# Sixteen gate tiles of block 1 moved to the first four turns, with later turns and a closer-packed norm

## The reference

```
h = RMSNorm(x);  P = h @ W_in     # q, k, v, og, low-rank decays, glu (value, gate), gA, gB
yA = (RMSNorm per head of GLA(q, k, v) * silu(og)) @ W_o
u  = glu_value * sigmoid(glu_gate)
yB = silu(LayerNorm(conv31(u))) @ W_pw2          # 31 taps, depthwise
x  = x + (sigmoid(gA) * yA + sigmoid(gB) * yB) @ W_out
x  = x + PEER(RMSNorm(x));  out = RMSNorm(x)
```

## Time and profile before

| | us |
|---|---|
| median of 3 runs | 4311.64 |
| lowest, highest | 4308.58, 4317.77 |
| the profiled execution, its own time | 4304.48 |
| its span in the trace | 4302.7 |

### The profile page before, as it was taken

How to read it: one execution, slowest core, us unless ns; L and a number is a source line. 1 busy time by engine, 2 the same in 40 slices (tenths; PEclk the granted TensorE clock), 3 DMA queues, 4 the chain that set the end, 5 groups by cost and what they waited for, 6 DMA issues and landing times. The chain is left out here.

```text
span 4302.7 us, 39452 instructions
## 1 busy us (share of the span) xinstructions
PE 3720.1 (86%) x13650; PEld 2238.9 (52%) x13650; DVE 2660.2 (62%) x3879; ACT 878.4 (20%) x2022; POOL 775.2 (18%) x525
## 2 busy tenths in 40 slices
PE   9999999999999989676799697858898887777777
PEld 3444489446666676573788586334444442322222
DVE  3232368103899999965777877876666664544444
ACT  2233210101122221241111111122222222212112
POOL 0000000000233323322221311321211121212111
PEclk9999999999999999898899898879999999999999
DMA  3111258888899999999999999999999999999998
GB/s 134 59 59 59 73 183 302 301 314 308 345 385 406 392 412 415 411 395 410 426 425 426 417 418 427 426 416 426 416 428 428 428 415 426 425 429 428 428 429 373
DMA packets 136877, 1530.03 MB, mean 356 GB/s; under 512 B 15297, under 2 KB 15425, under 8 KB 15937
## 3 DMA queue, kind: packets, MB, share of 16 engines
q0 software_dynamic: 73728, 1073.77, 59.3%
q1 hardware_dynamic: 61488, 445.33, 26.9%
q10 hardware_dynamic: 1552, 9.57, 0.6%
HBM read 1524.42 MB, written 4.19 MB: 355 GB/s over the span
## 5 line engine op out<-in xcount | busy, mean ns | idle before, releaser
L1773 PE MATMUL bank<-arena_h,wring 128*128 128x128 f32 (+5 forms) x6656 | 1384.0, 371 | 122.4 <-DVE arena_h L1471 41.7
L1773 PEld LDWEIGHTS bank<-arena_h,wring 128*128 128x128 f32 x6656 | 1026.0, 196 | 479.5 <-issue 188.5
L633 POOL DMA_INDIRECT arena_c<-in_peer_uv,arena_c x256 | 511.3, 1997 | 2469.7 <-DVE arena_o L1403 1320.0
L1394 DVE SCALAR_TENSOR_TENSOR arena_c<-arena_c 128x2048 f32<-128x2048 f32 x256 | 585.3, 2286 | 183.4 <-DMA arena_c<-in_peer_uv,arena_c 183.2
L2165 PE MATMUL bank<-arena_c,arena_h 128*128 128x512 f32 x1020 | 475.9, 610 | 156.7 <-ACT arena_h L1000 156.7
L1403 DVE SCALAR_TENSOR_TENSOR arena_o<-arena_c,arena_o 128x2048 f32<-128x2048 f32 x234 | 549.4, 2348 | 45.3 <-ACT arena_c L803 39.3
L2132 PE MATMUL bank<-arena_c,cols 128*128 128x512 f32 x1024 | 470.4, 602 | 95.8 <-ACT cols L958 93.8
L1670 DVE SCALAR_TENSOR_TENSOR arena_c<-arena_c 128x2048 f32<-128x2048 f32 x128 | 293.4, 2292 | 332.4 <-DMA arena_c<-in_peer_uv,arena_c 332.3
L801 ACT ACTIVATE arena_c<-arena_c 128x1 f32<-128x1 f32 x384 | 77.9, 203 | 1919.8 <-DVE arena_c L1394 1428.7
L646 POOL DMA_INDIRECT arena_c<-in_peer_uv,arena_c x256 | 261.8, 1023 | 1032.6 <-PE bank L2132 523.8
L1614 DVE SCALAR_TENSOR_TENSOR arena_c<-arena_c 128x2048 f32<-128x2048 f32 x128 | 293.4, 2292 | 238.7 <-DMA arena_c<-in_peer_uv,arena_c 237.8
(11 more groups left out here) (237 smaller groups left out, 2617.7 us busy)
## 6 DMA issues: line engine op xcount, KB each, us to landing
wring<-in_w_in SPq DMA_DIRECT2D x176, 1024.0 KB
wring<-in_w_out SPq DMA_DIRECT2D x48, 1024.0 KB
wring<-in_peer_w_q SPq DMA_DIRECT2D x48, 1024.0 KB
wring<-in_gla_w_o SPq DMA_DIRECT2D x32, 1024.0 KB
wring<-in_conv_w_pw SPq DMA_DIRECT2D x32, 1024.0 KB
wring<-in_w_v SPq DMA_DIRECT2D x16, 1024.0 KB
wring<-in_w_ga SPq DMA_DIRECT2D x16, 1024.0 KB
wring<-in_w_o_quarters SPq DMA_DIRECT2D x16, 1024.0 KB
```

Source lines behind the costliest of these rows:

```text
L633: pool.indirect_dma_start(out=slot_of(n), out_offset=None, in_=uv_tab, in_offset=at)\
L1394: V.scalar_tensor_tensor(row, row, 1.0, block_of(h2, n // P), ALU.mult, ALU.mult, accum_out=act_u[:, n % TOP:n % TOP + 1]).then_inc(dotted, 1)
L1773: last = M(ps[bank][:, at:at + hi - lo], w_tile(slot)[:, k, :], act_in[:, k, lo:hi], start=k == 0, stop=k == KT - 1)
```

## The change

- **Loads and TensorE.** Right after the first glu tiles come eight second gate tiles (`SB_GB0`, pairs 0 to 3), into banks 4 to 7, and then turn 0's output gates. Each of turns 0 to 3 keeps its pair (now pairs 4 to 7). The eight tiles between the last turn and the pointwise tiles are gone. So ten are made in turn 0 and two in each of turns 1 to 3.
- **Turns.** Turn 0 begins at step 6 instead of 4 and has 17 steps instead of 11; turns 1 to 3 begin 8 steps later with unchanged lengths (12, 11, 12); turns 4 to 7 have 9, 9, 8, 8 steps instead of 9, 9, 9, 8. The last tap falls before step 92 instead of 85.
- **Turn 0's places.** Its output gates are scaled at steps 8 and 11 of the turn. ScalarE's sigmoids of pairs 0 to 3 stand at steps 7 to 10, those of pairs 4 to 7 at the step of the second scaling.
- **Norm.** Subtractions and squares take two steps instead of four, four pairs of tiles and eight tiles a step. `RSTD_AT` is 6 steps after the last turn's end (7 before), the pointwise merges 8 (10), the residual additions 15, 16, 17, 18 (18, 20, 22, 24), the norm 19 (25), the queries 24 (30), the search 26 (32).
- **Semaphores.** TensorE waits for the sigmoids of banks 4 to 7 ahead of each output-gate tile, and at the end of a turn for that turn's sigmoid.

```diff
+SB_GB0 = SB_GLU1 + 4
+SB_OG1 = SB_GB0 + 8
...
-TURN_AT = (4, 15, 27, 38, 50, 59, 68, 77, 85)
+TURN_AT = (6, 23, 35, 46, 58, 67, 76, 84, 92)
 OG_AT = (4, 7)
+OG_AT_FIRST = (8, 11)
 IT_AT = (2, 5)
-X1_AT = 84
-GB_IN_TURN = 7
-GB_AT = (84, 86)
-XC_AT, SQUARE_AT = 88, 89
-RSTD_AT = 92
-PW_AT = 95
-SCALE2_AT, SILU2_AT = 96, 97
-RES1_AT = (103, 105, 107, 109)
-NORM1_AT = 110
-QUERY1_AT = 115
-FIND_AT = 5
+X1_AT = 91
+GB_FIRST_AT = (7, 8, 9, 10)
+XC_AT, SQUARE_AT = 95, 96
+RSTD_AT = 98
+PW_AT = 100
+SCALE2_AT, SILU2_AT = 101, 102
+RES1_AT = (107, 108, 109, 110)
+NORM1_AT = 111
+QUERY1_AT = 116
+FIND_AT = 6
...
             loads(SB_GLU1 + 2, 0, 4, w_in, WGLU, 2)
+            loads(SB_GB0, 0, 8, w_in, WGB, 8)
...
-                    loads(first + 4, i, 20, w_in, i * 4 + (WGB + 2 * turn), 2)
+                    loads(first + 4, i, 20, w_in, i * 4 + (WGB + 8 + 2 * turn), 2)
...
-            loads(SB_GB1, 0, 8, w_in, WGB + 8, 8)
...
-                A(sgb1[:, 2 * n:2 * n + 2, :], two(4 if n < 4 else 6 + n % 2, P), ACT.Sigmoid).then_inc(p["sig"], 1)
+                A(sgb1[:, 2 * n:2 * n + 2, :], two(4 + n if n < 4 else 4, P), ACT.Sigmoid).then_inc(p["sig"], 1)
...
-                    if j < 4 and r + 1 in OG_AT:
-                        og1_silu(j, OG_AT.index(r + 1))
-                    if j < 4 and r == GB_IN_TURN:
-                        mb1_gates(j)
+                    og_at = OG_AT if j else OG_AT_FIRST
+                    if j < 4 and r + 1 in og_at:
+                        og1_silu(j, og_at.index(r + 1))
+                    if j < 4 and r == og_at[1]:
+                        mb1_gates(4 + j)
...
-                if s in GB_AT:
-                    mb1_gates(4 + GB_AT.index(s))
-                if 0 <= s - SQUARE_AT < 4:
-                    for t in range(4 * (s - SQUARE_AT), 4 * (s - SQUARE_AT) + 4):
+                if s in GB_FIRST_AT:
+                    mb1_gates(GB_FIRST_AT.index(s))
+                if 0 <= s - SQUARE_AT < 2:
+                    for t in range(8 * (s - SQUARE_AT), 8 * (s - SQUARE_AT) + 8):
...
-                if s - SQUARE_AT in (2, 4):
-                    mb1_gates(5 + (s - SQUARE_AT) // 2)
...
-                if 0 <= s - XC_AT < 4:
+                if 0 <= s - XC_AT < 2:
...
-                    for g in range(2 * (s - XC_AT), 2 * (s - XC_AT) + 2):
+                    for g in range(4 * (s - XC_AT), 4 * (s - XC_AT) + 4):
...
             glu1(SB_GLU1, 0, 4, 0, 0)
+            for n in range(4):
+                two_tiles(SB_GB0 + 2 * n, None, 0, hT, 4 + n, P, 2 * P).then_inc(pair["mb1"]["gate"], 1)
             with pe.Fori(0, 2) as i:
                 for turn in range(2):
                     first = SB_OG1 + 10 * turn
                     for n in range(4):
+                        pe.wait_ge(pair["mb1"]["sig"], i * 2 + (turn + n + 1))
                         pe.wait_ge(og1["used"], i * 8 + (4 * turn + n + 1))
...
-                    pe.wait_ge(pair["mb1"]["sig"], i * 2 + (turn + 1))
+                    pe.wait_ge(pair["mb1"]["sig"], i * 2 + (turn + 5))
...
-            def mb1_gate(n):
-                if n >= 6:
-                    pe.wait_ge(pair["mb1"]["sig"], n - 1)
-                two_tiles(SB_GB1 + 2 * (n - 4), None, 0, hT, 6 + n % 2, P, 2 * P).then_inc(pair["mb1"]["gate"], 1)
-
             pe.wait_ge(pair["ma1"]["use"], 2 + 8)
-            for n in range(4, 6):
-                mb1_gate(n)
...
-                if n % 2:
-                    mb1_gate(6 + n // 2)
```

More of the change, by code:

```diff
@@ L67 @@
 SB_GLU1 = SB_WQ0 + 2 * PH
-SB_OG1 = SB_GLU1 + 4
+SB_GB0 = SB_GLU1 + 4
+SB_OG1 = SB_GB0 + 8
 SB_MA1 = SB_OG1 + 40
 SB_MA1_LAST = SB_MA1 + 36
-SB_GB1 = SB_MA1_LAST + 8
-SB_PW1 = SB_GB1 + 8
+SB_PW1 = SB_MA1_LAST + 8
 SB_OUT1 = SB_PW1 + 16
@@ L1479, in beside @@
                     r, steps = s - TURN_AT[j], TURN_AT[j + 1] - TURN_AT[j]
-                    if j < 4 and r in OG_AT:
-                        og1_scale(j, OG_AT.index(r))
+                    og_at = OG_AT if j else OG_AT_FIRST
+                    if j < 4 and r in og_at:
+                        og1_scale(j, og_at.index(r))
                     if j >= 4 and r in IT_AT:
```

## The result

The changed kernel took 4326.51 us (median of 6 runs, 4321.52 to 4341.75), the kernel before 4307.65 beside it (4301.61 to 4317.77): ratio 1.0046, 95% interval 1.0033 to 1.0059, 19 us slower. A second set of runs, later and on the same chip as the first experiments, gave 4325.99 against 4309.85: 1.0041 [1.0028, 1.0055], 16 us. The forecast was 4317.5 us, 9 us less: the time lies inside the range of 4301 to 4334, but beyond the 0.2% of the likeliest case. As a difference to before the miss is larger: +5.8 us was forecast, on a median of 4311.64 for the kernel before, and +19 and +16 were measured beside 4307.65 and 4309.85.

What follows compares the result with a forecast made beforehand. DMA bounds the kernel: bytes at 427 GB/s plus DMA time left unused earlier. Terms -14.2 + 2.3 + 17.7 = +5.8 us on the median of 4311.6 gave 4317.5 us, range 4301 to 4334.

Steps and rivals of the forecast that it cites:

- the likeliest case: Whole kernel: gain and loss nearly cancel, -3 to +13 us; under 0.2% (8.6 us) counts as no change; chance 0.52.
- Bound and method: Whole kernel: the end is the bytes at 427 GB/s plus DMA time left unused before about 2025 us.
- Turn 0, -14.2: Turn 0: eight more rows and eight tiles, 58.9 us of DMA, go early for 44.7 us of delay; gain 14.2 us.
- the fourth load starts when the first gate tile does: Turn 0: load starts at 1143.7, six tiles land 7.4 us apart, the last at 1188; TensorE starves 15.4 us.
- Turn 0 jams: Turn 0: ScalarE, held by gates, delays adds, rows and output gates, turn 1 by another 8 us; +14, 4325; chance 0.12.
- Turn 0 is worth more: Turn 0: tiles come every 3.65 to 4.9 us, gain 27 to 29 us; -9 us, 4303; chance 0.12.
- Turn 6, +2.3: Turn 6: 8 steps instead of 9, one row (4.91 us of DMA) less; loss 2.3 us, bounds 0.4 and 4.9.
- Turn 7 and norm, +17.7: Turn 7 and norm: 25.0 us of DMA work leaves, they last 7.3 us less; loss 17.7 us, bounds 12 and 25.
- Pointwise tiles, residual, next norm: From first pointwise tile on: DMA work per residual step just matches TensorE's 14.7 us; loss 0, bounded by 15 us.
- The packed tail idles: Successive residual adds: slots full while TensorE walks its tiles, squares hold ScalarE; 10 us more, +16, 4327; chance 0.24.
- The signs named ahead: Trace marks from turn 0 to step 111, such as TensorE idle 12 to 18 us and DMA above 400 GB/s.
- the two signs of being wrong: Norm's chain taking much over or under 56 us, or residual steps running well under 400 GB/s.

Runs made afterwards that it cites:

- steps-only: Later turns, packed norm and tail of the change on the kernel before, the eight gate tiles left in place; 4303.13 us, ratio 0.9989.

## Why the prediction was right in kind and wrong in size

- **Bound and method** (spare DMA time against the full rate): right; the ledger closes within 1 us, for before against the change and for steps-only against the change.
- **Turn 0, -14.2**: measured -10.3 with what turns 1 to 3 gained. The spacing of 7.4 us and TensorE's idle time (13.6 for 15.4) were right. The step that failed is "the fourth load starts when the first gate tile does [...] land 7.4 us apart": the first of those loads was issued 2.8 us later than forecast, and nothing of it moved for the next 2.6 us, so that its tile was used 11.1 us after the issue and not 7.4. The next take came at 1281.0 and not at 1276.5 (on the clock of before). ScalarE's hold was twice as long as I said, and harmless, as the run with later sigmoids showed. *Turn 0 jams* is thereby out, and *Turn 0 is worth more*, which needed TensorE to starve under 3 us, is out by the 13.6.
- **Turn 6, +2.3**: measured 2.3 in turns 4 to 6, though turn 6 itself lost nothing (2.4 before and after) and the whole of it lies in turns 4 and 5. That the sum fits is luck.
- **Turn 7 and norm, +17.7**: measured +15.6. Turn 7 at 369 GB/s for "near 370"; the norm at 303 for "near 280". Up to the first pointwise tile it moved 308 GB/s in 52.2 us, 16.1 MB; the forecast's 280 in 56 us is 15.7 MB, so the bytes were about right and the chain shorter.
- **Pointwise tiles, residual, next norm: "Just filled: 0"**: this is the step that made the likeliest case wrong. Measured +8.8: 1.6 there, 6.3 up to step 132, 0.9 after. The argument counted DMA work against TensorE's time over the whole stage, and that balance was about right (7.9 spare for 6.3). It left out the state in which the stage hands over: slots full, weights loaded ahead, no request outstanding (359 GB/s in the next 40 us, where before had 425). The second rival, *The packed tail idles*, had the mechanism (slots full while TensorE walks its tiles) and near enough the price: 10 us for 8.8. That its 4327 meets the 4326.51 measured is luck: it stands on a before of 4311.64 and adds no miss in turn 0. That the packed places cost by themselves is shown: +10.6 with everything else as before, +4.1 for the residual additions alone.
- **The signs named ahead.** Four came: TensorE's 13.6 us idle, 407 GB/s from 1147 to 1273 (1144 to 1270 on the clock of before), turn 7's rate, and the first pointwise tile 35.5 us later. Three missed: the second take of values at 1281.0 for 1274 to 1279, the norm's rate, and step 111 at 2041.6 (clock of before) for 2030 to 2035. Of the two signs of being wrong, the one on the residual steps came true: 386 GB/s.

The misses sum as 3.9 + 0 - 2.1 + 8.8 = 10.6, which is 16.4 - 5.8.

What the argument didn't separate is which part earns and which costs. It booked turn 0's gain as a joint one, 58.9 us of rows and tiles for 44.7 us of time. The runs split it: rows alone, with the tail's price, -6.7; tiles on top, +22.9. Before, TensorE is never idle in turns 0 to 3, and a tile placed there lengthens a stage that TensorE bounds. In turn 7 VectorE bounds: it had 69.6 us of work in each of these kernels, and the turn lasted 73.3 us with the four tiles in it (steps-only) and 70.8 without, while DMA fell to 369 and 370 GB/s wherever they were gone.

Moving four of the eight costs nothing that can be told (4300.9 against 4303.13, each known to about 4 us), moving eight 22.9. The stages shown above say why. With the steps alone moved, turns 0 to 3 last 121.4 + 261.6 = 383.0 us, VectorE is busy nearly all of it, and TensorE has 14.46 us of room. Four tiles fill that room: turns 1 to 3 still last 261.6 us, TensorE now busy 259.79 of them instead of 247.14, and turn 0 grows by 5.3 us, 3.04 of them a wait for a tile. With eight, TensorE is busy all of turns 1 to 3, which last 271.2 us while VectorE still has only 261.56 us of work, and turn 0 lasts 138.6 us with 13.6 us of waits for tiles. Together that is 21.5 us more than with four. Between the profiles of four and eight moved, spare differs by 13.9 us (5.6 in turn 0, 7.4 in turns 1 to 3, 2.6 in turn 7 and norm, 1.7 the other way in the rest) for 14.3 us of span, but the medians differ by 25, since the profiled execution with four was 8 us above its median. What the other executions with four did better is not shown; the profile of four is 6 us longer than that of steps-only.

## What to carry to other kernels

Count idle time of the binding resource stage by stage, and ask of each filler what bounds the stage that it leaves and the one that it enters: a tile is free only where its own engine isn't the bound, and only up to that engine's room (here 14.46 us, four tiles). Count the state at which a stage hands over (slots full, nothing outstanding), not only its own balance, since a backlog is what keeps the next stage at the full rate. And split a change that moves two things before keeping or dropping it: here one half was worth keeping.

## What the runs showed of the hardware

- A weight load issued while a gather was being moved saw its first packet 2.6 us later, and its tile was used 11.1 us after the issue. Loads that followed one another came 7.4 us apart. Once both queues moved, they took turns packet by packet: 153 to 153 for that load, 287 to 287 a little later, 1555 to 1558 in the steady window.
- In the norm TensorE's granted clock was 0.71, where it was 0.85 before. It was 1.00 while TensorE summed the last squares (1878.0 to 1884.3). After 11.23 us idle the first pointwise tile ran at 0.50, the lower of the two levels (1895.5 to 1899.8), and at 1.00, the upper, from 1906.0 to 1912.0.
